# An encoder layer with retrieved experts: row sums in three portions, even token groups, merges in pieces

## The reference

```python
h = rmsnorm(x, g_mix)
z = h @ w_in                     # [pool 512 | q 512 | k 128 | v 128 | gate_pool 1024 | gate_attn 1024]
pool_branch = pool_mixer(p, pool_w, pool_scale) @ w_pool_out
attn_branch = gqa_attention(rope(rmsnorm(q)), rope(rmsnorm(k)), v) @ w_attn_out   # 8 heads, 2 kv heads
x = x + (sigmoid(gate_pool) * pool_branch + sigmoid(gate_attn) * attn_branch) @ w_out
h = rmsnorm(x, g_ffn)
q = (h @ w_query).reshape(C, 8, 2, 128)                  # 8 heads, two halves each
s = einsum('chpd,hpkd->chpk', q, sub_keys)               # 128 scores for each half
sv, si = top_k(s, 16)                                    # the 16 best of each half
top_s, pos = top_k(all 256 sums of a pair of halves, 16) # the 16 best pairs of each head
idx = ids of these pairs, out of 16384 experts           # 128 experts for each token
gate = softmax(top_s)
hid = gelu(einsum('cd,chkd->chk', h, expert_u[idx])) * gate
x = x + einsum('chk,chkd->cd', hid, expert_v[idx])
y = rmsnorm(x, g_final)
```

## Time and profile before

| | |
|---|---|
| median of 3 runs | 2984.92 us (2981.93 to 2986.37) |
| profiled execution, own time | 2985.82 us |
| its span | 2984.0 us |
| mean granted TensorE clock | 0.951 of full speed |
| busy: PE / DVE / POOL / ACT | 2620.7 / 2071.2 / 1526.6 / 481.9 us |

### The profile page before, as it was taken

The page is one execution under the profiler, slowest core; times in us unless marked ns, Lnnn a source line. Parts: engine busy times, 40 slices in busy tenths (PEclk is TensorE's granted clock), DMA queues, the critical chain, the costliest instruction groups (busy, mean ns, idle before and its releaser), DMA issues.

```text
span 2984.0 us, 30618 instructions
## 1 busy us (share of the span) xinstructions
PE 2620.7 (88%) x9973; PEld 1499.7 (50%) x9973; DVE 2071.2 (69%) x4568; ACT 481.9 (16%) x910; POOL 1526.6 (51%) x1284
## 2 busy tenths in 40 slices
PE   7989868879978889767589899999999999999997
PEld 6785546535634465334255444444444455444543
DVE  1437876686087768456688977977777777777778
ACT  2321601120136014122130000010000000000001
POOL 0002574455455750222525566776666676666675
PEclk9999989989989999889799999999999999999999
DMA  4376897788787984666898999999999999999998
GB/s 155 114 233 216 274 381 289 264 316 293 278 299 254 368 305 132 215 205 208 285 324 335 375 384 410 392 378 396 410 410 411 408 405 410 407 410 409 408 410 317
DMA packets 361185, 961.55 MB, mean 322 GB/s; under 512 B 28000, under 2 KB 152672, under 8 KB 359008
## 3 DMA queue, kind: packets, MB, share of 16 engines
q0 software_dynamic: 184320, 671.17, 59.5%
q1 hardware_dynamic: 126048, 259.52, 23.9%
q10 hardware_dynamic: 50688, 29.36, 3.3%
HBM read 930.58 MB, written 29.36 MB: 322 GB/s over the span
## 4 chain that ended last, share of the span: by engine, by line
PE 31%; DMA 28%; issue 17%; DVE 16%; POOL 5%; ACT 3%; POOLq 0%; DVEq 0%; ACTq 0%; SPq 0%
PE bank L615 17%; DMA ring<-in_expert_v,idx 15%; DMA ring<-in_expert_u,idx 12%; PE bank L603 6%; POOL ring L1234 5%; DVE ring L1269 5%; PE o_bank L632 3%; DVE region_a L1286 3%; DVE consts L1640 2%; PE bank L668 1%; ACT region_s L1034 1%; DVE neg_max L1358 1%; DVE consts L1634 1%; PE bank L593 1%; DVE region_q L1530 1%
## 5 line engine op out<-in xcount | busy, mean ns | idle before, releaser
L1234 POOL DMA_INDIRECT ring<-in_expert_u,idx x640 | 781.5, 1221 | 753.4 <-DVE idx L1541 315.1
L1234 POOL DMA_INDIRECT ring<-in_expert_v,idx x640 | 744.9, 1164 | 684.0 <-PE o_bank L632 397.1
L1269 DVE CUSTOM_DVE_ANT_0 ring<-ring,h 128x1024 f32<-128x1024 f32 x640 | 766.0, 1224 | 184.0 <-DMA ring<-in_expert_u,idx 177.9
L892 PE MATMUL bank<-wslot,gate_attn 128*128 128x512 f32 x1536 | 705.8, 610 | 70.4 <-DVE gate_attn L1577 66.1
L882 PE MATMUL o_bank<-region_b,wslot 128*128 128x384 f32 x2048 | 681.3, 486 | 1.9 <-DVEq L1610 1.9
L1286 DVE SCALAR_TENSOR_TENSOR region_a<-ring,dots,region_a 128x1024 f32<-128x1024 f32 x384 | 493.1, 1284 | 152.8 <-DMA ring<-in_expert_v,idx 130.0
L882 PEld LDWEIGHTS o_bank<-region_b,wslot 128*128 128x128 f32 x2048 | 389.0, 190 | 300.8 <-issue 63.1
L892 PEld LDWEIGHTS bank<-wslot,gate_attn 128*128 128x128 f32 x1536 | 295.9, 195 | 438.7 <-issue 327.0
L1141 ACT ACTIVATE gate_attn<-o_bank 128x384 f32<-128x384 f32 x128 | 62.7, 490 | 1287.7 <-PE o_bank L882 1254.4
L632 PE MATMUL o_bank<-ring,gate_attn 128*32 128x512 f32 x1024 | 146.5, 698 | 112.5 <-DMA ring<-in_expert_v,idx 105.2
L615 PE MATMUL bank<-region_b,wslot 128*128 128x128 f32 (+2 forms) x768 | 231.7, 459 | 2.8 <-ACT region_b L928 2.8
(11 more groups left out here) (171 smaller groups left out, 1901.6 us busy)
## 6 DMA issues: line engine op xcount, KB each, us to landing
wslot<-in_expert_uT SPq DMA_DIRECT2D x128, 512.0 KB
wslot<-in_expert_v SPq DMA_DIRECT2D x128, 512.0 KB
wslot<-in_w_in SPq DMA_DIRECT2D x34, 1024.0 KB
wslot<-in_w_query SPq DMA_DIRECT2D x24, 1024.0 KB
expert_weights<-region_p ACTq DMA_DIRECT2D x24, 1024.0 KB
wslot<-in_w_out SPq DMA_DIRECT2D x12, 1024.0 KB
region_s<-expert_weights SPq DMA_DIRECT2D x8, 1536.0 KB
region_p<-expert_weights SPq DMA_DIRECT2D x8, 1536.0 KB
```

What stands on the lines that cost most here:

```text
L892: ins = nc.tensor.matmul(dense_out[2 * t + n][:], hidden[q][:, t * P:(t + 1) * P], v_cols[slot][:, n * 512:(n + 1) * 512], start=start, st ...
L1234: nc.gpsimd.indirect_dma_start(ring[:, n % RING, :], None, expert_u if what == "u" else expert_v, bass.IndirectOffsetOnAxis(ap=ids, axis=0 ...
L1269: nc.vector.tensor_tensor_reduce(row, row, h2[:, H2_AT[k], :], 1.0, 0.0, ALU.mult, ALU.add, dots[:, DOTS_AT[k] + s:DOTS_AT[k] + s + 1]).th ...
```

## The change

- Groups: batch 0 is worked as tiles (0,1) and (2,3) instead of one and three.
- Batch 1: its x is loaded into `region_a` as soon as group 1 has read it for the last time, and it is squared and normed within the queries of group 1. In group 2 the order on PE is heads, pool, gates, where it was gates, pool, heads.
- Sums: the 32 quads of (0,0) are split into 20 (behind pool projections, gates and `pool_out`) and 12 (behind `gate_attn` and `attn_out`); the 32 of (0,1) form the third portion, one quad at steps 0, 1 and 3 of each query step c and eight behind `w` jobs. Each portion has its own zeroed weights, and its own `add_sums`.
- Rows: the order of the ring mixes v rows of (0,0) and u rows of (0,1), in runs of 8 v and 10 u, later 8 v and 5 u.
- DVE: `dot` calls are spread anew (3 and 4 in place of 6 and 3; 2 behind each half of group 1, and the last 40 in one piece); `merge(0, 2)` is interleaved with the steps of `attn_out` of group 2, `merge(0, 3)` with those of `out`; `merge(1, 3)` is done for six heads and then for two. Softmax is taken tile by tile. One activation tile, (1,1), is computed a second time later on (`norm2_again`).

```diff
-GROUP_OF = ((0, (0,)), (0, (1, 2, 3)), (1, (0, 1, 2, 3)))
+GROUP_OF = ((0, (0, 1)), (0, (2, 3)), (1, (0, 1, 2, 3)))
-GATHERS = [("u", 0), ("v", 0), ("u", 1), ("v", 1), ("u", 2), ("u", 3), ("u", 4), ("v", 2), ("v", 3), ("v", 4)]
-ROW = {key: n * SLOTS for n, key in enumerate(GATHERS)}
+def gather_order():
+    rows = lambda what, k, first, count: [(what, k, s) for s in range(first, first + count)]
+    yield from rows("u", 0, 0, SLOTS)
+    yield from rows("v", 0, 0, V_FIRST)
+    u, v = 0, V_FIRST
+    for groups, each, alone in ((GROUPS_BEFORE, U_BEFORE, U_BETWEEN), (GROUPS_AFTER, U_AFTER, U_LAST)):
+        for _ in range(groups):
+            yield from rows("v", 0, v, 8)
+            yield from rows("u", 1, u, each)
+            u, v = u + each, v + 8
+        yield from rows("u", 1, u, alone)
+        u += alone
+    yield from rows("v", 1, 0, SLOTS)
...
+V_FIRST, GROUPS_BEFORE, U_BEFORE, U_BETWEEN, GROUPS_AFTER, U_AFTER, U_LAST = 40, 5, 10, 30, 6, 5, 18
-SUMS_AT = {("query", 1, 4): 2, ("query", 1, 5): 2, ("query", 1, 6): 2, ("query", 1, 7): 2, ("hT",): 2,
...
+SEGMENTS = (
+    (0, {**{("p", c, tp): 1 for c in range(2) for tp in range(2)}, ("pooled",): 1, ("mixed",): 1,
+         **{("gate_pool", d): 2 if d % 4 == 3 else 1 for d in range(KD)}, **{("pool_out", d): 1 for d in range(1, KD, 2)}}),
+    (0, {("attn_out", 1): 1, ("gate_attn", 2): 1, ("gate_attn", 3): 1, ("attn_out", 3): 2, ("gate_attn", 4): 1,
+         ("gate_attn", 5): 1, ("attn_out", 5): 1, ("gate_attn", 6): 1, ("gate_attn", 7): 1, ("attn_out", 7): 2}),
+    (1, {**{("query", c, step): 1 for c in range(KD) for step in (0, 1, 3)},
+         **{("w", n): 1 for n in range(66, 96, 4)}}))
...
             for hp in range(HALVES):
                 top_halves(1, hp)
-                if hp < 5:
-                    dot(4)
-                if hp == 5:
-                    weigh(0)
-            norm1(1)
+                dot(2)
+                if hp == HALVES // 2:
+                    norm1(1)
+            dot(SLOTS - dotted[0])
+            weigh(0)
+            square_heads(1)
             merge(0, 1)
-            merge(0, 2)
-            turn_ids(2, 1)
-            merge(0, 3)
-            rotate(1)
-            pool_out(2, 2)
+            rotate(1, 4)
+            pool_out(2, 4)
             add_sums(0)
-            split_ids(0)
             attention(2, 1)
-            attn_out(2, 6)
-            out(2, 4)
+            zero_sums(1)
+            todo = iter(range(KD))
+            def attend():
+                attn_out_step(2, next(todo))
+                dot(4)
+            merge(0, 2, attend)
+            zero_sums(2)
+            steps = out_steps(2)
+            def add_out():
+                next(steps)
+                dot(2)
+            merge(0, 3, add_out)
+            for _ in steps:
+                pass
+            add_sums(1)
             norm2(2)
             weigh(1)
+            turn_ids(2, 1)
+            softmax(2)
+            split_ids(0)
...
+                if c == HALVES // 2 - 1:
+                    merge(1, 3, first=0, last=PEER_HEADS - 2)
             for hp in (HALVES - 2, HALVES - 1):
                 top_halves(2, hp)
-            merge(1, 3)
+            merge(1, 3, first=PEER_HEADS - 2)
...
-            add_sums(1)
-            norm2_again(4)
+            add_sums(2)
+            for k in AGAIN:
+                norm2_again(k)
```

More of the change, by code:

```diff
@@ L152, in jobs_of @@
     elif g == FIRST_GROUP[1]:
-        yield from gates + pool + heads
+        yield from heads
+        yield (g, "wT", 0), None
+        yield from pool + gates
     else:
@@ L452, in all_used @@
         def all_used(eng, key):
-            for n in range(ROW[key] + SLOTS - RING, ROW[key] + SLOTS):
+            last = {}
+            for s in range(SLOTS):
+                last[ROW[(*key, s)] % RING] = ROW[(*key, s)]
+            for n in last.values():
                 used(eng, n)
@@ L623, in sum_rows @@
                     return
-                k, quads = SUMS_OF[key]
+                part, quads = SUMS_OF[key]
+                k = SEGMENTS[part][0]
+                if part and quads[0] == SUM_FIRST[part]:
+                    pe.wait_ge(sums_added, part)
                 for r in quads:
-                    rows = [ROW["v", k] + QUARTERS * r + q for q in range(QUARTERS)]
+                    rows = [ROW["v", k, QUARTERS * r + q] for q in range(QUARTERS)]
                     for n in rows:
                         landed(pe, n)
-                    pe.wait_ge(sum_w_ready, k * QUADS + r + 1)
+                    pe.wait_ge(sum_w_ready, SUM_BASE[part] + r - SUM_FIRST[part] + 1)
                     for half in range(2):
@@ L647, in turn_weights @@
                 pe.wait_ge(weighed, k + 1)
-                bank = fill(g, "wT")
-                done(nc.tensor.transpose(bank[:, 0:P], dots[:, DOTS_AT[k]:DOTS_AT[k] + SLOTS], ident[:]), g, "wT")
+                bank = fill(g, "wT", k)
+                done(nc.tensor.transpose(bank[:, 0:P], dots[:, DOTS_AT[k]:DOTS_AT[k] + SLOTS], ident[:]), g, "wT", k)
             def turn_chosen(d):
@@ L1080, in stores @@
                             store_weights(n)
+                        weigh_sums("query", c, step)
                 for c in range(HALVES // 2):
@@ L1149, in finish @@
                     if k < EARLY:
-                        act.wait_ge(sums_added, k + 1)
+                        act.wait_ge(sums_added, max(part for part in range(len(SEGMENTS)) if SEGMENTS[part][0] == k) + 1)
                     else:
@@ L1316, in rotate @@
                 dve.sem_inc(head_sq_ready, 1)
+            def rotate(b, rows=0):
                 dve.wait_ge(head_std_ready, b + 1)
@@ L1427, in out @@
                 dve.sem_inc(x1_ready, 1)
+            def out(g, rows=0):
+                for _ in out_steps(g):
+                    dot(rows)
             def norm2(g):
@@ L1468, in top_halves, with candidates @@
                 ins.then_inc(halves_done, 1)
-            def candidates(out, first, second):
+            def candidates(out, first, second, count):
                 for a, rows, cols, off in CAND_RUNS:
@@ L1502, in merge @@
                 pause()
-                ns = [step(nc.vector.max(top[:, h, 0:8], cand[:, h, :])) for h in range(PEER_HEADS)]
+                ns = {h: step(nc.vector.max(top[:, h, 0:8], cand[:, h, :])) for h in range(first, last)}
                 pause()
-                for h in range(PEER_HEADS):
+                for h in range(first, last):
                     after(ns[h])
@@ L1521, in merge @@
                 found = sel_f[:, PEER_HEADS:, :]
-                link(nc.vector.tensor_copy(pos, pos_i))
+                link(nc.vector.tensor_copy(pos[:, heads], pos_i[:, heads]))
                 hits = [m.rearrange("p (k n) -> p k n", n=CAND) for m in match]
                 ns = [n_dve[0]] * 2
-                for h0 in range(0, PEER_HEADS, 2):
+                for h0 in range(first, last, 2):
                     pause()
@@ L1599, in weigh, with add_sums @@
                 dve.wait_ge(weighed, k + 1)
-            def add_sums(k):
+            def add_sums(part):
+                k = SEGMENTS[part][0]
                 b, t = GATHERED[k]
-                all_used(dve, ("v", k))
+                for q in range(QUARTERS):
+                    used(dve, ROW["v", k, QUARTERS * SUM_LAST[part] + q])
                 for half in range(2):
@@ L1675, in _ @@
             merge(0, 0)
-            pool_out(1, 1)
+            pool_out(1)
             attention(1, 1)
-            attn_out(1, 6)
-            out(1, 3)
-            dot(4)
+            attn_out(1, 3)
+            zero_sums(0)
+            out(1, 4)
             norm2(1)
```

429 lines of the change are left out of this document (232 added, 197 removed).

## The result

The changed kernel takes 3071.99 us (median of 4 runs, 3069.59 to 3093.52), the kernel before beside it 2985.64 (2981.93 to 2992.71): a ratio of 1.030, 95% interval 1.025 to 1.035. The profiled execution has a span of 3071.7 us. Forecast were 3006 us, range 2930 to 3050: the direction holds, the size does not, and the time lies outside the range.

What follows compares the result with a forecast made beforehand. Before the constant, DMA-filled last part, PE is busiest but nowhere full, held by DVE and v rows. Against 2985.8 us, +12 +58 +17 -47 -18 = +22 gives 3008, and the median, 0.9 lower, 3006; range 2930 to 3050.

Steps and rivals of the forecast that it cites:

- Constant last part, 1402 us: From the first late row to the end: rows, columns and order stay alone, so it keeps taking 1402 us.
- First u row at 365, and PE's idle time ahead of the turned weights: Before batch 1's pool: first u row 99 us later, at 365; PE waits some 25 us for 40 dots, until 642.
- Quad 10 at 735: Behind batch 1's first pool jobs and four pool gates: the tenth quad is used at about 735 us.
- Cycles of 30 us, quad 10 to quad 18 in 120: Before attention of group 2: four cycles of 18 rows, two exchanges each, at 30 us; attention starts at 885, 12 later.
- `gate_attn` and `attn_out` 150 us: Attention's end to `out`, group 2: six cycles of 13 rows, 150 us instead of 92, 58 later; bounds 105 and 165.
- `Out` to queries +17: From `out` to the first query job of group 2: DVE's added work makes it 93.5 us instead of 76.6, 17 later.
- Queries -47: Queries of group 2: single quads need not wait, steps take 31 us; 246 us instead of 293, 47 earlier.
- Behind them -18: Behind the queries, up to the first late row: waits for PE's queued quads go; 18 us earlier.
- rival B: Queries of group 2: quads still wait 3 us each, 72 us, the 47 gained are lost; 3055 us, chance 0.13.
- Rival A: Mixed stretches before `out`: a quad's exchange is short, 8 us; 66 us earlier in total, 2940 us, chance 0.27.
- Rival C: Whole kernel: gains and losses cancel within a few us, stops in the gates cost 20 less; 2985 us, chance 0.10.
- The signs named beforehand: Between 735 and 885 us: some 8 PE waits for v rows, together 50 us or more; DVE waits for u rows.

Runs made afterwards that it cites:

- ring of six: The changed kernel with a ring of 6 rows instead of 8: 3215.18 us, ratio 1.076 to the kernel before.
- half rows: The changed kernel with rows of tiles (0,0) and (0,1) bringing 512 of their 1024 elements, same number of rows: 3024.50 us, ratio 1.012 to the kernel before.
- half runs: The changed kernel with 4 v and 5 u rows by turns before attention, 4 v and 2 u behind it: 3055.99 us, ratio 1.024 to the kernel before.

## Why the prediction was right and wrong, step by step

- **Constant last part, 1402 us**: right, 1402.8.
- **First u row at 365, and PE's idle time ahead of the turned weights**: the row right, 367.0. The idle time was 33.8 us instead of 25, and the turning came at 654.7 instead of 642: DVE began the 40 dots at 593.6 and not 589, and took 59 us for them, 1.48 each, inside the bounds of 46 and 73 but above the 51 taken. (How 589 follows from 501 and 79, the prediction does not say; with their sum, 580, it would have been 9 us lower still.) Undoing the groups took 18.7 us away at this point and 35.0 of the span, so this step is real.
- **Quad 10 at 735**: 18 late, at 753.3. The 13 us above are most of it.
- **Cycles of 30 us, quad 10 to quad 18 in 120**: this is the step that failed. They took 149.6 us (753.3 to 902.9), 37.4 each. I priced an exchange by one quad in a burst, 3.7 us of issues and 8 of flight, and counted two of them and the dots. The flight was right: 7.5 us in the mean. What is missing is POOL's issues in their order. The v rows of the next quad stand behind ten u rows: in the round shown the last of them is the 14th issue from 789.94 on, with a stop of 4.9 us behind the fourth and 1.58 us for each of the last ten where the earlier trace rows have 1.24. That is 25.4 us before the last flight of 8.3 begins and the slow quad of 3.6, where I had 19 to 23. In the next round the stop of 13.65 us for DVE's dots comes on top, which I had not counted either. What PE did in between did not hide it. The sum is +53 before attention instead of +12: 18 from the late start, 30 from the cycles, 7 less behind quad 18.
- **`gate_attn` and `attn_out` 150 us**: the same step, 177.4, +85 instead of +58. It lies outside even the bounds of 105 and 165. Without u rows it is 118.7, so the mix costs 59 us, where I had 45 for stops. What I had called the end of the stretch, 12 us of DVE behind with `merge(0, 2)`, was worth less: moved away, the stretch is 4.8 us shorter.
- **`Out` to queries +17**: +18.7. **Queries -47**: -53. **Behind them -18**: -17. All right, and rival B with its 72 us of waits in the queries is out: PE's last wait for v rows lies before 1174, and the queries pass three quads in 30 us without one. (B's own sum was off: 3006 and 72 are 3078, and 3055 is the forecast with only the 47 lost.)
- **Rival A, a short exchange**, is out: the loaded flight was 6.6 to 9.2 us, not 4.5. **Rival C**, where gains and losses cancel, is out with the total.

The two mis-sized terms are 41 and 27 us too small, 68 together, and the other three together 3 too large; that makes up the error of 66 within a microsecond. (The terms as written add up to 3007, not 3006.) The signs named beforehand were there in kind, larger than told: PE waited 75 us for v rows between 735 and 903 where 50 or more were named. What I wrote while experimenting went wrong in a second way: that the runs' length was the cause. Halving them gave 16 us; the 159 us are the price of having two readers' rows pass in stretches where PE needs a v row every 2.1 us. Of the rate of 2 us a row, the runs show that slots (ring of six), flight (half rows) and the order (half runs) each take part. The rest, 1.4 to 1.5 us a row, is POOL issuing one row after another by its timeline; no run changes that alone, so that its share is read and not tried.

A page of the Trainium skill stood beside this term. "DMA: Bandwidth & Descriptors", the anatomy of one DMA on the SWDGE path, has 2.0 us plus bytes / 436e3, by which halving a row of 524288 bytes would save 0.6 us (an estimate from the page). The half rows saved 2.8 us of the time from issue to use (7.5 to 4.8 in the mean of five waits, 9.2 to 6.2 in the round shown), so under this load the trace does not agree with it.

## What to carry to other kernels

A ring that one engine fills in order is shared by its readers: before moving a second reader's rows into a stretch, divide its length by its rows, both readers' together, and compare that with the rate which the same ring shows with such readers under load (here 1.4 us a row for DVE alone, 2.0 to 2.3 with PE's quads), not with the flight of a lone group. And count, for the row that a reader waits for, all issues that stand ahead of it in the order. Spread transfers into stretches where the ring idles, as the third portion does (60 rows in 294 us before), and leave full ones alone. And a wait that goes away is worth nothing where another engine's chain lies beside it: the burst under `rotate` was free, and the merge pieces under the waits for u rows cost 5 of their 33 us.

## What the runs showed of the hardware

- An issue of an indirect row took POOL 0.94 us, and up to 1.99 in the mixed stretches, in a mean of 1.15; halving the row's bytes left the mean at 1.13, though the DMA engines fell from 288 to 178 GB/s. So the bytes are not what stretches it; what does stays open.
- The time from a row's issue to its use was 4.5 us on quiet queues, 7.5 in the mean of five waits before attention at 288 GB/s, and 4.8 there with half the bytes.
- A wait costs PE twice. Between 655 and 913 us its granted clock was 0.83, and 0.98 in the run without the u rows; before attention the quads behind waits of 8 to 18 us took 3.64 us, those between two jobs 1.92.
- Two executions of one stretch of the same instructions (60 to 120 us) had the clock at 0.89 and at 1.00, and stood 10 us apart at 490 us. What makes them differ stays open.
